# The first two output tiles of each layer moved into the last slots of its attention

## The reference, cut to what matters

```python
# layer 0: causal differential attention, 8 heads of 128 columns
o = diff_causal_attention(q, k, v, lam, slopes_a)
o = rms_norm(o, a_subln_g[l]) * (1.0 - lambda_init)
o = o.reshape(bsz, seq, A_INNER) * jax.nn.silu(z)
h = h + gate * (o @ a_w_out[l])          # the output stage of layer A
k_s, v_s = ...                           # from rms_norm(h) @ w_kv
# layer 1: sliding-window attention, 16 heads of 64 columns
u = rms_norm(h, b_norm_g[l]) * (1 + scale) + shift
o = o.reshape(bsz, seq, B_INNER) * jax.nn.silu(z)
h = h + gate * (o @ b_w_out[l])          # the output stage of layer B
```

## Time and profile before

| | before |
|---|---|
| median of 3 runs | 1236.7 us (1235.08 to 1238.17) |
| the profiled execution | 1240.81 us, span 1239.0 us |
| mean granted clock of PE | 0.961 |
| PE busy | 1141.4 us (92% of the span) |
| DVE / ACT / POOL busy | 730.4 / 668.9 / 172.7 us |
| moved by DMA | 107.92 MB, 87 GB/s on average |

### The profile page before, as it was taken

How to read it: one execution, slowest core, us unless ns; L and a number is a source line. 1 busy time by engine, 2 the same in 40 slices (tenths; PEclk the granted TensorE clock), 3 DMA queues, 4 the chain that set the end, 5 groups by cost and what they waited for, 6 DMA issues and landing times.

```text
span 1239.0 us, 18959 instructions
## 1 busy us (share of the span) xinstructions
PE 1141.4 (92%) x5920; PEld 883.9 (71%) x5920; DVE 730.4 (59%) x2344; ACT 668.9 (54%) x2039; POOL 172.7 (14%) x305
## 2 busy tenths in 40 slices
PE   1478999999999999999978999689999999998997
PEld 1356777777777777777756888568877788787886
DVE  7676767767677676767663545545555555555221
ACT  3665565656666565655652555546656666664010
POOL 1510011111111010111100111121111111110212
PEclk9688999999999999999988999889999999996999
DMA  9621222323222223222213332300111111123342
GB/s 367 207 79 49 84 77 83 95 68 95 68 85 76 102 72 94 84 77 84 69 41 140 119 121 67 119 18 27 43 48 39 40 39 49 42 57 119 119 136 85
DMA packets 51125, 107.92 MB, mean 87 GB/s; under 512 B 5584, under 2 KB 18000, under 8 KB 50896
## 3 DMA queue, kind: packets, MB, share of 16 engines
q1 hardware_dynamic: 51024, 106.70, 27.1%
HBM read 89.90 MB, written 16.78 MB: 86 GB/s over the span
## 4 chain that ended last, share of the span: by engine, by line
PE 81%; DVE 7%; issue 5%; ACT 4%; DMA 2%; POOL 1%; POOLq 0%; DVEq 0%; SPq 0%; ACTq 0%
PE ps_p L517 15%; PE ps_p L519 13%; PE ps_p L518 13%; PE ps_s L549 6%; PE ps_o L599 5%; PE ps_p L690 4%; PE ps_p L691 4%; PE ps_p L692 4%; PE ps_o L659 3%; PE ps_t L612 3%; PE ps_s L643 2%; PE ps_t L675 2%; PE ps_o L714 2%; PE ps_o L575 1%; PE ps_t L704 1%
## 5 line engine op out<-in xcount | busy, mean ns | idle before, releaser
L517 PE MATMUL ps_p<-w_hi,u_hi 128*128 128x512 f32 x768 | 338.7, 441 | 19.9 <-DVE u_lo L1047 19.9
L519 PE MATMUL ps_p<-w_hi,u_lo 128*128 128x512 f32 x768 | 305.7, 398 | 0.0
L518 PE MATMUL ps_p<-w_lo,u_hi 128*128 128x512 f32 x768 | 304.7, 397 | 0.0
L517 PEld LDWEIGHTS ps_p<-w_hi,u_hi 128*128 128x128 f32 x768 | 147.1, 192 | 84.2 <-ACT gbuf L777 28.6
L519 PEld LDWEIGHTS ps_p<-w_hi,u_lo 128*128 128x128 f32 x768 | 146.6, 191 | 33.5
L518 PEld LDWEIGHTS ps_p<-w_lo,u_hi 128*128 128x128 f32 x768 | 147.9, 193 | 17.6
L826 ACT ACTIVATE e<-e,negm 128x256 f32<-128x256 f32 (+7 forms) x128 | 98.3, 769 | 98.6 <-DVE negm L1100 97.5
L998 DVE TENSOR_TENSOR w_lo<-raw,w_hi 128x512 fp32r<-128x512 f32 x120 | 82.5, 695 | 92.5 <-ACT w_hi L750 92.3
L451 POOL TENSOR_SCALAR gbuf<-gbuf 128x128 f32<-128x128 f32 (+1 forms) x96 | 36.6, 381 | 569.5 <-ACT gbuf L777 569.5
L549 PE MATMUL ps_s<-kT,qT 64*128 64x512 f32 (+3 forms) x384 | 90.2, 547 | 7.2 <-DVE negm L1100 4.6
L750 ACT ACTIVATE w_hi<-raw 128x512 fp32r<-128x512 f32 x128 | 79.0, 629 | 11.8 <-DMA raw<-w_a 7.9
(11 more groups left out here) (161 smaller groups left out, 2039.1 us busy)
## 6 DMA issues: line engine op xcount, KB each, us to landing
adabuf<-ada_w SPq DMA_DIRECT2D x48, 512.0 KB, 3.9
raw<-w_a SPq DMA_DIRECT2D x80, 256.0 KB, 3.9
raw<-w_b SPq DMA_DIRECT2D x48, 256.0 KB, 3.1
ada_in<-ada_w SPq DMA_DIRECT2D x7, 1024.0 KB, 14.3
x_in<-x SPq DMA_DIRECT2D x8, 512.0 KB, 7.3
oa_scratch<-gbuf SPq DMA_DIRECT2D x64, 64.0 KB, 1.6
e<-oa_scratch SPq DMA_DIRECT2D x8, 512.0 KB, 3.6
stage<-x SPq DMA_DIRECT2D x8, 512.0 KB, 5.1
```

The costliest lines, as they stand in the source:

```text
L517: pe.matmul(o, u_hi[:, c, t], w_hi[par][:, c, :], start=(c == 0), stop=False)
L518: pe.matmul(o, u_hi[:, c, t], w_lo[par][:, c, :], start=False, stop=False)
L519: mm = pe.matmul(o, u_lo[:, c, t], w_hi[par][:, c, :], start=False, stop=(c == KD - 1))
```

## The change

The row loads no longer go into `e0` but into `late`, a view of the space of `u_lo`: 128 columns of each of its eight 1024-column rows, so that one load writes eight pieces of 512 bytes per partition (before: one piece of 4 KB). With `e0` out of the way, the two first loads are issued in SP's drain slot 1 as soon as the last projection has read `u_lo`. PE transposes row tile 0 in drain slot 2, into `ps_p`, and row tile 1 in drain slot 3, into `ps_t`; `half(0, 0)` stands in drain slot 3 behind `gate_rows` and ahead of the last PV, `half(0, 1)` in drain slot 4. ACT and DVE make the parts of tiles 0 and 1 in drain slots 2 and 4. The output stages begin at step 2. Both layers are changed alike. The products, transposes and transfers are the same in number; where they stand and how the loads are cut up changes.

```diff
+        late = over(u_lo_at, "late", [P, KD, SEQ])
...
+        def rows_in_u(n):
+            return late[:, :, (5 + n % 2) * P:(6 + n % 2) * P]
+
+        def rows_psum(n):
+
+            return flat(ps_p[:, :, :]) if n == 0 else ps_t[:, :]
...
@@ -334,14 +344,15 @@
+                    if not live(0) and i == 1:
+
+                        sp.wait_ge(S.proj, units * NT)
+                        for k in range(2):
+                            sp.wait_ge(S.st[k], 16 * ((units - 1) * NT // 2 + 1))
+                            sp.dma_start(rows_in_u(k), groups(o_dram[k * P:(k + 1) * P, :], P)).then_inc(c_o[k], 16)
                     if not live(0) and i < 4:
                         for c in (2 * i, 2 * i + 1):
                             load_chunk(units + 1 + unit0, c, w_src[units + 1, :, c, :])
-                    if not live(0) and i == 4:
-                        sp.wait_ge(S.pt, units * (UNIT_CHUNKS if is_a else NT))
-                        for k in range(2):
-                            sp.wait_ge(S.st[k], 16 * ((units - 1) * NT // 2 + 1))
-                            sp.dma_start(e0[:, k, :], o_dram[k * P:(k + 1) * P, :]).then_inc(c_o[k], 16)
...
@@ -591,6 +625,7 @@
                     if not live(0) and i == 3:
                         pe.wait_ge(S.m, 2 * units * UNIT_CHUNKS)
                         gate_rows(gate)
+                        out_half(n0, unit_out, 0, 0)
...
+                    if not live(0) and i == 2:
+
+                        pe.wait_ge(S.ez, units * NT)
+                        pe.wait_ge(S.qn, units * NT)
+                        out_rows(n0, 0)
...
+                    if not live(0) and i == 3:
+                        pe.wait_ge(S.phi, units * NT)
+                        out_rows(n0, 1)
+                    if not live(0) and i == 4:
+                        out_half(n0, unit_out, 0, 1)
...
@@ -675,35 +726,20 @@
-                for s in range(NT + (4 if with_next else 1)):
+                for s in range(2, NT + (4 if with_next else 1)):
...
@@ -853,6 +902,8 @@
                     split_for(S, u, i, par, live, units, U_A)
+                    if not live(0) and i in (2, 4):
+                        transposed(n0, i // 2 - 1)
```

More of the change, by code:

```diff
@@ L541, in gate_rows, with out_rows, out_half, attn_a @@
                 mm.then_inc(g_mm, 1)
-            def attn_a(S, units, gate):
+            def out_rows(n0, n):
+                m = n0 + n
+                pe.wait_ge(c_o[n % 2], 16 * (m // 2 + 1))
+                at_least(pe, c_lo, 2 * m)
+                for d in range(KD):
+                    mm = pe.transpose(rows_psum(n)[:, d * P:(d + 1) * P], rows_in_u(n)[:, d, :], ident[:, :])
+                    if d % 4 == 3:
+                        mm.then_inc(c_tr, 1)
+            def out_half(n0, unit, n, h):
+                m = n0 + n
+                at_least(pe, c_y, 2 * (m - 1) + h + 1)
+                for c in range(KD):
+                    if h == 0 and c % 4 == 0:
+                        pe.wait_ge(c_lo, 2 * m + c // 4 + 1)
+                    if n == 0:
+                        w_ready(pe, unit + h, c)
+                    hi, lo = rows_t(n, 0)[:, c, :], rows_t(n, 1)[:, c, :]
+                    pe.matmul(ps_p[:, h, :], hi, w_hi[h][:, c, :], start=(c == 0), stop=False)
+                    pe.matmul(ps_p[:, h, :], hi, w_lo[h][:, c, :], start=False, stop=False)
+                    mm = pe.matmul(ps_p[:, h, :], lo, w_hi[h][:, c, :], start=False, stop=(c == KD - 1))
+                mm.then_inc(c_mm, 1)
+            def attn_a(S, units, gate, n0, unit_out):
                 def scores(u, it, n, part):
@@ L677, in slot @@
                     part_of_projection(range(7, KD))
+                    if not live(0) and i == 3:
+                        pe.wait_ge(S.phi, units * NT)
+                        out_rows(n0, 1)
+                    if not live(0) and i == 4:
+                        out_half(n0, unit_out, 0, 1)
                 all_units(pe, units, 5, slot)
             def output(n0, unit, with_next):
[L681 to L693, removed]
-                for s in range(NT + (4 if with_next else 1)):
+                for s in range(2, NT + (4 if with_next else 1)):
                     n1, n2, n3, n4 = s - 1, s - 2, s - 3, s - 4
-                    if 0 <= n1 < NT:
-                        half(n1, 0)
+                    if n1 < NT:
+                        out_half(n0, unit, n1, 0)
                     if s < NT:
[L700 to L706, removed]
+                        out_rows(n0, s)
                     if with_next and 0 <= n3 < NT:
@@ L1174, in slot @@
                     split_for(u, i, par, live, units, U_A)
+                    if not live(0) and i in (2, 4):
+                        transposed(y_done, i // 2 - 1)
                     if first and i >= 2:
@@ L1269, in output @@
                 chain = 0
-                for s in range(NT + (4 if with_next else 1)):
+                for s in range(1, NT + (4 if with_next else 1)):
                     n1, n2, n3, n4 = s - 1, s - 2, s - 3, s - 4
```

62 lines of the change are left out of this document (37 added, 25 removed).

## The result

The changed kernel took 1219.8 us (median of 4 runs, 1218.6 to 1224.4) against 1236.9 beside it (4 runs, 1235.1 to 1238.2): a ratio of 0.987, 95% interval 0.985 to 0.989, 17.1 us less. Forecast were 10.5 us less and 1226.2 us, so the direction was right, and the time lies 1.2 us under the range of 1221.0 to 1232.0. Two later measurements of the same kernel gave 0.986 [0.984, 0.989] at 1222.0 us and 0.988 [0.985, 0.992] at 1223.8, inside the range; the gains of the three, 17.1, 15.7 and 13.5 us (mean 15.4), all exceed the forecast.

What follows compares the result with a forecast made beforehand. PE, busy for 92% of the span, was taken to bound the kernel. Gains of 5.7 us in layer A and 4.8 in layer B made 10.5, taking the median from 1236.7 to 1226.2 us, range 1221.0 to 1232.0.

Steps and rivals of the forecast that it cites:

- What bounds the kernel: PE, busy 92% of the span: work moved earlier at an output stage's head comes off the end unless a wait eats it.
- I take 2.3 for the new hole: Layer A, PE idle before normed tile 0: low clock behind it costs 2.3 us, leaving a gain of 5.7.
- the clock stays up: Rival: full clock over layer A's new hole, cut in two of 1.4 and 0.9 us; gain 12.8, 1223.9 us, chance 0.22.
- V: The end of layer A's last PV, from which the later steps of its output stage are counted; forecast 659.0 to 661.1.
- All holes of 1.7 us and more were followed by the low clock: Reading of the profile before: PE waits of 1.74, 4.75 and 1.81 us were each followed by low clock.
- PV now ends at 659.0 to 661.1 instead of 655.14: Layer A: the last PV, queued behind half(0, 0), ends later; called the price of the change.
- Layer B: PE's list at the second join: gain 4.3 to 5.3 us, middle 4.8; 2.3 if the clock stayed low through half(0, 0).
- The small pieces: Row loads in pieces of 512 bytes: 0.4 us more per load, covered by other work.
- The median: Profiled 1240.81 us less 10.5 gives 1230.3; it lay 4.1 above the median, so 1236.7 goes to 1226.2 us.
- the clock falls more often: Rival: low clock at layer A's new hole and through B's half(0, 0), late V in A; gain 6.1, 1230.6 us, chance 0.20.
- no change: Rival: earlier start given back because tile 0's norm hangs on the residual; decides at V = 668.1; 1236.7 us, chance 0.05.
- slower: Rival: small-piece row loads come late for every tile, from 23.5 us a load in output B; 1241 us, chance 0.03.

Runs made afterwards that it cites:

- stretched hole: Changed kernel with the 1 MB load of the next weights issued ahead of tile 0's residual load in layer A's output; 1227.9 us, 0.992 of the kernel before.
- the loads alone: Kernel before with only the row loads changed in both layers: early, in pieces of 512 bytes; 1235.5 us, 0.998 of the kernel before.
- the filled one: Changed kernel, half(0, 0) behind the last PV, gate product in drain slot 4, nine unread matmuls in drain slot 1; 1216.5 us, 0.983 of the kernel before.

## Why the prediction was too small

**What bounds the kernel** held: PE sets the pace, and work moved up at the head of an output stage came off the end, 15.0 us for both layers one by one and 15.7 together.

**Layer A, the clock.** "I take 2.3 for the new hole" is the first step that failed, and rival *the clock stays up* had it right. The hole came, in two pieces as the rival said, 0.57 and 0.73 us instead of the 1.4 and 0.9 reckoned: row load 2 landed when forecast (V + 13.6 against V + 13.3), but PE came to it 1.1 us later, as told below. In none of the four profiles in which layer A is changed as proposed did the clock fall behind it. The stretched hole did cost 1.5 us, so I was right that a long hole there loses the clock, and wrong to charge a loss seen behind 1.74 us and more to two pieces of which each is shorter. "All holes of 1.7 us and more were followed by the low clock" was itself too strict, as the section at the end shows.

**Layer A, V.** This is the second step that failed. "PV now ends at 659.0 to 661.1 instead of 655.14", 3.9 to 6.0 us later. Counted from the store, the last PV ended at 22.6, 21.0 and 22.3 us in kernels before and at 23.8, 25.1, 23.8 and 25.3 in changed ones: 2.5 us later in the mean, 2.4 less than the middle of my range. It failed at `gate_rows`: I let it run at full or at half clock and took the middle. In the change it ran at the full clock in three of four profiles (1.95 us, 2.84 in the fourth); with the old hole it took 3.57, 3.62 and 3.62, and 2.74 with the loads alone. Part of that is luck: in three of the four a wait of 2.02 us still stood ahead, and the last section shows that the clock may or may not fall behind it. I also counted on the half clock that the profile of before happened to have ahead of it (the last PV but one took 2.98 us); in the profile of the stretched hole, which has nearly the same (2.94), V comes 3.9 us later than in the profile of before, the lower end of my range. From V on the forecast was close: transposes of the normed tile at V + 15.1, measured V + 15.4; the sum, released by the residual, at V + 9.0, measured V + 9.3; `half(1, 0)` at V + 6.4, measured V + 7.3.

That last 0.9 is a wait that I had missed: the gate product that frees `ps_p` stands in DVE's queue behind tile 1's low part and two small products, so PE stood 0.99 us for `adabuf`. It cost nothing at the end, since the normed tile was waited for anyway.

With both, and 0.3 less for the longer way from V on, 5.7 + 2.3 + 2.4 − 0.3 = 10.1, against 10.3 measured in the mean of the profiles and 9.0 timed with layer A alone.

**Layer B** gave 5.66 us in the two profiles and 6.0 timed, 4.8 forecast with 5.3 as the upper end. The half clock over its head stayed as I assumed; `gate_rows` took 2.45 us to the next instruction, the short one of my two values, which gives the upper end of 5.3; the remaining 0.4 is spread over rows that I had rounded up.

**The small pieces** cost less than the 0.4 us a load that I worked out from the rows: at most 0.04 us a tile, and nothing in two profiles. A window over the row load of tile 4 shows mostly 341 to 351 GB/s in its middle, and the load landed 3.9 us after issue; the fixed costs that the Trainium skill's page "DMA: Bandwidth & Descriptors" names in "Why small descriptors are slow (HBM only)" can't be seen behind work that hides them:

```profile
GB/s 0 0 0 0 0 0 0 0 0 0 0 0 0 39 161 63 122 180 312 341 346 351 341 346 346 341 351 317 332 405 346 283 137 234 273 78 390 156 78 429
...
late<-oa_scratch SPq DMA_DIRECT2D x1, 512.0 KB, 3.9
```

**The median.** I subtracted the gain from a profile that lay 4.1 us above its median and carried the distance over. That was sound: the 4.1 us at the head came and went in either kernel. The joins give 10.3 + 5.7 = 16.0 and the three measurements 15.4 in the mean; that the first reads 17.1 may be its share of short heads, but its unprofiled runs leave no trace that shows it.

Of the other rivals, *the clock falls more often* came true at neither of its places (new hole of A, `half(0, 0)` of B), V of the changed kernels, 657.1 on the count of the profile of before (632.58 + 24.5), stayed 11 us short of the point at which *no change* decides (668.1), and *slower* needed row loads of 23.5 us where the slowest seen in output B took 6.9.

## What to carry to other kernels

Where the clock of TensorE falls behind holes, a hole costs more than its length: here 6 us came back by filling holes with matmuls that nothing reads, and 7 to 10 of the change's 16 were faster matmuls, and a forecast that only moves work misses them. When a change fills a hole, cost what runs behind it at the full clock first and keep the low clock for the range, rather than take the middle; and when it makes new holes, compare them in length with the shortest one that a row shows losing the clock, piece by piece (here 1.71 us against 0.57 and 0.73). Count the profile of before from an event near the change, and look for stretches at half clock that it has by chance: one profile is one throw.

## What the runs showed of the hardware that I had not expected

Behind one and the same wait the clock falls in some runs and not in others. The 2.02 us wait ahead of the last softmax transposes left `gate_rows` at 1.95 us in two profiles, and at 2.84, 2.86 and 3.06 in three others. A 2.4 us wait in layer B's drain was followed by half clock in nine profiles (for some 13 us in the profile after) and by none in three others, worth some 5 us. Ahead of the softmax transposes of drain slot 1 of layer A every kernel but the filled one waits 2.55 us; in the profile after the four score matmuls behind it run at the full clock:

```profile
632.29 1.07 PE L652 MATMUL ps_t<-ident,e 128*128 128x128 f32 x7 [2.55 <-DVE e L1224]
633.30 1.13 PE L583 MATMUL ps_s<-kT,qT 64*128 64x512 f32 x4
```

and in the profile of the stretched hole the same four take 2.08:

```profile
636.46 1.75 PE L673 MATMUL ps_t<-ident,e 128*128 128x128 f32 x7 [2.56 <-DVE e L1248]
638.15 2.08 PE L601 MATMUL ps_s<-kT,qT 64*128 64x512 f32 x4
```

The shortest wait seen just ahead of such a fall is 1.71 us, for the row load of layer B in the second profile of the kernel before (1.74 in the earlier trace rows). What decides between the cases no run here shows.
